# Index keys and query latents projected first, their norms and the gate chain run inside the in-projection

## The chip, the cores and the metric

The kernel runs on one core of one Trainium2 chip. Time is device microseconds (us) of one execution; the median of three runs is the metric. The engines are TensorE (PE; its weight loads are PEld), VectorE (DVE), ScalarE (ACT), GpSimd (POOL) and SyncE (SP, which issues the DMA transfers here).

## The reference, cut to what matters

One decoder layer over 512 tokens of width 1024. One input projection feeds two groups of heads:

```python
h = rms_norm(x, ln1_g[l])
proj = h @ w_in[l]
gq, gk, gv, gz, ga, gb, cq, ckv, kidx, widx = jnp.split(proj, offsets, axis=-1)
o_a = gdn_mixer(gq, gk, gv, gz, ga, gb, conv_w[l], a_log[l], dt_bias[l], gdn_norm_g[l])
o_b = dsa_mixer(cq, ckv, kidx, widx, q_norm_g[l], kv_norm_g[l], w_q_up[l], w_qidx_up[l],
                w_kv_up[l], idx_ln_g[l], idx_ln_b[l], rel_bias)
...
# gdn_mixer
qkv = jax.nn.silu(causal_depthwise_conv(jnp.concatenate([q, k, v], axis=-1), conv_w))
q = l2_normalize(q...); k = l2_normalize(k...)
g = -jnp.exp(a_log) * jax.nn.softplus(a + dt_bias)
beta = jax.nn.sigmoid(b)
o = gated_delta_rule(q, k, v, g, beta)
o = rms_norm(o, norm_g) * jax.nn.silu(z)
# dsa_mixer
cq = rms_norm(c_q, q_norm_g);  q_idx = (cq @ w_qidx_up);  ckv = rms_norm(c_kv, kv_norm_g)
k_idx = layer_norm(k_idx, idx_ln_g, idx_ln_b)
w_idx = w_idx * (IDX_HEADS ** -0.5 * IDX_DIM ** -0.5)
```

After these come the gated delta rule in chunks of 64, the index scores with a top-k choice, the attention, the output projection, and an expert network (PEER) that takes most of the time.

## The kernel before

The program is a row of blocks. All five engines enter a block together and leave it together; inside, each runs its own list in order, and semaphores join them. This case is about the first block (`in_stage`) and the start of the second (`mixer_stage`); everything behind is left alone.

`in_stage` computes 21 tiles of 128 output channels by 512 tokens. For tile `i` SP loads 512 KB of weights, ScalarE rounds them to a high part (`split(i)`, L212), VectorE makes the low part (`w_rest(i)`, L283), and TensorE runs three passes of 8 matmuls (L362, L374, L379). `split(i)` may start when tile `i-2` is done, since there are two weight buffers. Bank `i % 4` holds the result; ScalarE stores it (`store`, L216; the first four on VectorE, L287). The tile order is that of the rows of `proj`: tiles 0 to 11 are q, k, v of the delta rule, 12 to 15 its gate z, 16 to 19 the query and key/value latents (`CQ0`, `CKV0`), 20 the index keys together with the columns a, b and w_idx (`KI0`).

Between tiles the q, k, v rows are convolved on VectorE (`convolve`, L298 and L301), passed through Silu and squared on ScalarE (`convolved`), summed over partitions on TensorE (L386), given an inverse root by ScalarE's Ln and Exp (`roots`, L239 and L241) and scaled on VectorE (`normalise`, L305). Ln, Exp and Silu lie in three activation tables; a change between them is an ACT_TABLE_LOAD. Copy and Square need no load. Where a tile index matters: `roots(k)` waits for `normalise(2k-1)`, and TensorE waits for the Ln of `roots` before it reuses the banks of L386.

`mixer_stage` opens with a chain that needs tile 20 and the latents. TensorE transposes the index-key tile (L1147) and subtracts the mean (L1149); VectorE and ScalarE make from a and b the decay `g` and `beta` (L814 to L850); TensorE sums the squares of the four latents and of the centred keys (L1152 to L1155), multiplies the relative bias by the buckets (L1157, the `strip`), and sums `g` (L1159 to L1162, `cums`). Only then comes the loop over four heads: `row_sums(h)` (L1170 to L1173), `products(h)` (transposes L1181, then the 64-wide products L1189), the head's masks on VectorE (L886 to L892), the index projections `up_project` (L1227) and a transpose of the result (L1265). The norms of the latents and keys (L865 to L870) stand on VectorE inside the first head.

The head of TensorE's list in this block, in the code's own words:

```python
pe.wait_ge(s["rel"], 32)
mm(t.bank[0][0:H, :], rel[:], buckets[:, 0:T], start=True, stop=True).then_inc(s["strip"], 1)
...
pe.wait_ge(s["strip_s"], 2)
row_sums(0)
pe.wait_ge(s["llog"], 3)
products(0)
```

Of the kernel before, what the change touches and what calls it, by code (L numbers as in the profile page):

```python
# [27 lines left out]
P = 128  # L28
T = 512
# [24 lines left out]
NPROJ = 21  # L54
NEG = -1e30
# [107 lines left out]
def in_stage(t, a, x, proj, conv, hi, lo, x_hi, x_lo, sq, spare, parts):  # L163

    nc = t.nc
    LEAD = 4
    loaded = [t.sem(f"in_loaded{s}") for s in range(2)]
# [6 lines left out]
        t.sem("conv_" + k) for k in ("zeroed", "taps", "silu", "squared", "summed", "rooted", "inverted", "normed"))  # L176
    whi, wlo = (parts[:, k:k + 4, :].rearrange("p (s c) t -> p s (c t)", s=2) for k in (0, 4))
    raw = spare[:, 8:12, :].rearrange("p (s c) t -> p s (c t)", s=2)
    root, inv = spare[:, 12:14, :], spare[:, 14, :]
    slots = [proj[:, NPROJ - DC + c, PAD:PAD + T] for c in range(DC)]  # L180
# [4 lines left out]
    dest = lambda i: proj[:, i, PAD:PAD + T]  # L185
    bank = lambda i: t.bank[i % 4]
    with nc.Block() as block:

        @block.sync
        def _(sp):  # L190
# [10 lines left out]
            sp.dma_start(t.cst[:, rest], a["constants"][:, rest]).then_inc(rest_in, 16)  # L201
# [3 lines left out]
        def _(act):  # L205
# [24 lines left out]
            def gate(j):  # L230
                act.wait_ge(stored, j + 1)
                f(dest(j), dest(j), ACT.Silu).then_inc(silu, 1)

            def roots(k):
# [6 lines left out]
                f(both, both, ACT.Exp, scale=-0.5).then_inc(conv_inverted, 1)  # L241

# [21 lines left out]
            for i in range(6, NPROJ):  # L264
                u = i // 2
# [12 lines left out]
        def _(dve):  # L278
            tt, stt = nc.vector.tensor_tensor, nc.vector.scalar_tensor_tensor
# [13 lines left out]
            def convolve(j):  # L293
                dve.wait_ge(stored, j + 1)
                for tap in range(CONV):
                    w = v[:, V_CONV + j * CONV + tap:V_CONV + j * CONV + tap + 1]
                    if tap == 0:
                        nc.vector.tensor_scalar(conv[:, j, :], proj[:, j, 0:T], w, None, ALU.mult).then_inc(taps, 1)  # L298
                    else:
                        dve.wait_ge(taps, CONV * j + tap)  # L300
                        stt(conv[:, j, :], proj[:, j, tap:tap + T], w, conv[:, j, :], ALU.mult, ALU.add).then_inc(taps, 1)  # L301

            def normalise(j):
                dve.wait_ge(conv_inverted, j // 2 + 1)
                stt(conv[:, j, :], conv[:, j, :], v[:, V_QK + j:V_QK + j + 1], root[:, j % 2, :],  # L305
                    ALU.mult, ALU.mult).then_inc(conv_normed, 1)

# [22 lines left out]
            convolve(0)  # L330
            w_rest(5)
            store(3)
            convolve(1)
            for i in range(6, NPROJ):
# [5 lines left out]
            normalise(2 * H - 1)  # L340

# [7 lines left out]
        def _(pe):  # L349
            mm = nc.tensor.matmul  # L350
            for i in range(NPROJ):
                s = i % 2
                pe.wait_ge(w_high, i + 1)
# [5 lines left out]
                for c in range(DC):  # L359
                    if fresh:  # L360
                        pe.wait_ge(high_made, c + 1)
                    mm(bank(i)[:], whi[:, s, of_c[c]], highs[:, c, :], start=c == 0, stop=False)  # L362
                    if i == 0:
                        pe.wait_ge(low_made, c + 1)
                        mm(bank(i)[:], whi[:, s, of_c[c]], lows[:, c, :], start=False, stop=False)
                pe.wait_ge(w_low, i + 1)
                if i == 1:
                    pe.wait_ge(ones_in, 16)
                    for k in range(DC // 2):
                        pe.wait_ge(paired, k + 1)  # L370
                        last = mm(t.bank[4][:], t.c(C_ONES), sq[:, 2 * k + 1, :], start=k == 0, stop=k == DC // 2 - 1)
                    last.then_inc(added, 1)
                for c in range(DC):
                    last = mm(bank(i)[:], wlo[:, s, of_c[c]], highs[:, c, :], start=False, stop=i == 0 and c == DC - 1)  # L374
                if i:
                    for c in range(DC):
                        if fresh:
                            pe.wait_ge(low_made, c + 1)
                        last = mm(bank(i)[:], whi[:, s, of_c[c]], lows[:, c, :], start=False, stop=c == DC - 1)  # L379
                last.then_inc(summed, 1)  # L380
                j = i - 10
                if 0 <= j < 2 * H:
                    pe.wait_ge(conv_squared, j + 1)
                    if j >= 2:
                        pe.wait_ge(conv_rooted, j // 2)
                    mm(t.bank[6 + j % 2][:], t.c(C_ONES), sq[:, j, :], start=True, stop=True).then_inc(conv_summed, 1)  # L386
# [212 lines left out]
def mixer_stage(t, proj, conv, mix, hi, lo, qy, raw, front, tail, first_tiles, a_in):  # L599
# [11 lines left out]
        "chain", "ab_t", "ab", "exps", "u1", "log",  # L611
        "g", "beta", "below", "after", "cums", "g_col", "decays", "beg", "gl", "grow", "exp3", "tiles_t", "kk",
        "taken", "qk", "a", "a_t", "at", "prep", "mt", "x", "xs", "tx", "level", "u_t", "w_t", "u", "w", "zero",
        "ws", "vnew", "out", "o_copy", "ds", "state", "osq", "ossq", "olog", "oinv", "delta_mixed",
        "lsq", "mean", "centred", "csq", "lsum", "llog", "linv", "latents", "kin")}
    s.update({n: t.sem("dsa_" + n) for n in (
        "wqi", "wq", "wkv", "rel", "w_idx", "up", "up_out", "strip", "strip_s", "strip_out",
# [24 lines left out]
    with ExitStack() as ctx:  # L642
# [4 lines left out]
        ab = sb("ab", [P, NB, 8])  # L647
        small = sb("small", [P, 16, 16])
        ghalf = sb("ghalf", [P, 2, 16])
# [6 lines left out]
        w_idx = sb("w_idx", [P, NB, IH])  # L656
# [13 lines left out]
        gl, eg = tmp[:, 0, half0], up_q[:, 0, :]  # L670
# [4 lines left out]
        latent = [proj[:, CQ0 + i, PAD:PAD + T] for i in range(4)]  # L675
        keys_i = proj[:, KI0, PAD:PAD + T]
        sm = [small[:, i, :] for i in range(16)]
# [1665 lines left out]
```

## Time and profile before

| | before |
|---|---|
| median of 3 runs | 1635.97 us (1634.32 to 1637.51) |
| the profiled execution's own time | 1635.17 us |
| its span | 1633.4 us |
| mean granted TensorE clock | 0.990 |
| TensorE matmul busy | 1571.5 us (96%) |
| VectorE / ScalarE / GpSimd busy | 1301.6 / 701.4 / 604.4 us |

The span runs from the first instruction to the last; the 1.8 us beside it lie outside the trace. The in-projection fills the first 141 us, and the head loop of the mixer lies between 151 and 196 us. Rows of the timeline give the start, the duration of the merged piece, the engine, the line and the operation; in brackets stands how long the engine was idle before it and what ended that. Matmul durations overlap, so the distance between starts is the better price. A float32 matmul of the mixer appears as two records.

### The profile page before, as it was taken

How to read it: one execution, taken by the hardware profiler on the slowest of the kernel's cores; microseconds unless marked ns; L12 is line 12 of the kernel's file. 1: busy time of each engine (PE TensorE's matmuls, PEld its weight loads, DVE VectorE, ACT ScalarE, POOL GpSimd, SP SyncE). 2: the span in 40 equal slices, each digit the busy share in tenths (PEclk: the TensorE clock that was granted, in tenths of full speed). 3: DMA queues.
4: the chain of work that ended last, by engine and by line, in shares of the span. 5: the costliest groups of instructions: out<-in, count | busy, mean ns of one | idle time of the engine just before them, and what ended most of it. 6: DMA issues, size and time to landing. Idle time of an engine off the chain costs nothing.

```text
span 1633.4 us, 26769 instructions
## 1 busy us (share of the span) xinstructions
PE 1571.5 (96%) x9253; PEld 1362.2 (83%) x9253; DVE 1301.6 (80%) x2391; ACT 701.4 (43%) x1118; POOL 604.4 (37%) x447
## 2 busy tenths in 40 slices
PE   7998889879999999999999999999999999999997
PEld 5876576558789999999999999998888888888886
DVE  6844567876525989999999999758898989898887
ACT  6474357363433334343444444433333333333334
POOL 3000047155402678787533333223333333322220
PEclk9999999989999999999999999999999999999999
DMA  4321011002243588888899999999999999999995
GB/s 135 114 69 60 2 41 27 26 27 90 89 157 101 174 269 290 270 282 293 254 334 362 347 343 349 345 345 397 381 381 399 379 380 387 392 360 338 360 367 192
DMA packets 149112, 404.47 MB, mean 248 GB/s; under 512 B 14176, under 2 KB 71776, under 8 KB 145568
## 3 DMA queue, kind: packets, MB, share of 16 engines
q1 hardware_dynamic: 108704, 243.93, 43.7%
q0 software_dynamic: 36864, 134.23, 21.5%
q10 hardware_dynamic: 3456, 25.17, 3.7%
q8 instruction: 51, 0.84, 0.2%
q14 instruction: 37, 0.30, 0.0%
HBM read 350.77 MB, written 52.51 MB: 247 GB/s over the span
## 4 chain that ended last, share of the span: by engine, by line
PE 56%; DVE 11%; issue 1%; ACT 0%; DMA 0%; POOL 0%; DVEq 0%; ACTq 0%
PE bank L1614 32%; PE bank L2148 7%; PE bank L2152 7%; PE bank L2149 7%; DVE own_waste L1930 3%; PE bank L2170 3%; DVE back L1981 1%; DVE rt_num L1952 1%; DVE rt_num L1945 1%; DVE rt_work L1946 1%; DVE rt_pos L1974 0%; DVE rt_pos L1971 0%; DVE rt_cand L1964 0%; DVE back L2002 0%; DMA h<-u_rows_dram,own_experts 0%
## 5 line engine op out<-in xcount | busy, mean ns | idle before, releaser
L1614 PE MATMUL bank<-rt_u_parts,rt_w_hi 128*128 128x512 f32 x1536 | 369.1, 389 | 0.0
L2148 PE MATMUL bank<-hi_parts,rt_u_parts 128*128 128x384 f32 x1024 | 349.5, 341 | 0.0
L2149 PE MATMUL bank<-lo_parts,rt_u_parts 128*128 128x384 f32 x1024 | 342.4, 334 | 0.0
L1614 PEld LDWEIGHTS bank<-rt_u_parts,rt_w_hi 128*128 128x128 f32 x1536 | 288.1, 188 | 59.8
L1843 ACT ACTIVATE rt_u_parts<-raw 128x1024 fp32r<-128x1024 f32 x126 | 133.8, 1062 | 336.7 <-PE bank L2152 296.8
L1480 ACT ACTIVATE rt_u_parts<-raw 128x1024 fp32r<-128x1024 f32 x128 | 135.9, 1062 | 320.9 <-PE bank L1614 293.2
L2199 POOL DMA_INDIRECT h<-u_rows_dram,own_experts x128 | 177.3, 1385 | 224.2 <-DVE own_waste L1930 210.0
L2205 POOL DMA_INDIRECT qy<-v_dram,own_experts x128 | 130.9, 1023 | 347.3 <-DVE qy L1554 341.4
L1890 POOL TENSOR_TENSOR rt_u_parts<-raw,rt_u_parts 128x1024 fp32r<-128x1024 f32 x66 | 163.3, 2474 | 127.0 <-ACT rt_u_parts L1843 125.6
L1536 DVE TENSOR_TENSOR rt_u_parts<-raw,rt_u_parts 128x1024 fp32r<-128x1024 f32 x128 | 156.7, 1224 | 66.4 <-ACT rt_u_parts L1480 64.2
L2152 PE MATMUL bank<-hi_parts,rt_u_parts 128*128 128x384 f32 x1024 | 198.4, 334 | 1.2 <-DVE rt_u_parts L1923 1.2
L1614 PE MATMUL bank<-rt_u_parts,rt_w_lo 128*128 128x512 f32 x768 | 194.9, 389 | 0.0
L2149 PEld LDWEIGHTS bank<-lo_parts,rt_u_parts 128*128 128x128 f32 x1024 | 192.6, 188 | 0.0
L2148 PEld LDWEIGHTS bank<-hi_parts,rt_u_parts 128*128 128x128 f32 x1024 | 192.5, 188 | 0.0
L2152 PEld LDWEIGHTS bank<-hi_parts,rt_u_parts 128*128 128x128 f32 x1024 | 179.3, 188 | 1.5 <-DVE rt_u_parts L1923 1.5
L1614 PEld LDWEIGHTS bank<-rt_u_parts,rt_w_lo 128*128 128x128 f32 x768 | 144.1, 188 | 29.9
L1554 DVE SCALAR_TENSOR_TENSOR qy<-qy,own_weights 128x1024 f32<-128x1024 f32 x128 | 163.9, 1280 | 0.1
L1930 DVE SCALAR_TENSOR_TENSOR own_waste<-h,bank 128x1024 bf16<-128x1024 f32 x104 | 126.6, 1218 | 4.7 <-DMA h<-u_rows_dram,own_experts 2.0
L1923 DVE TENSOR_TENSOR rt_u_parts<-raw,rt_u_parts 128x1024 fp32r<-128x1024 f32 x60 | 73.5, 1226 | 31.4 <-ACT rt_u_parts L1843 31.4
L1536 DVE TENSOR_TENSOR rt_w_lo<-rt_w,rt_w_hi 128x384 fp32r<-128x384 f32 x128 | 70.6, 552 | 0.7 <-ACT rt_w_hi L1484 0.7
L480 DVE TENSOR_TENSOR conv_parts<-proj,conv_parts 128x1024 fp32r<-128x1024 f32 x22 | 32.7, 1485 | 48.0 <-ACT conv_parts L432 48.0
L1484 ACT ACTIVATE rt_w_hi<-rt_w 128x384 fp32r<-128x384 f32 x128 | 65.4, 511 | 11.5 <-DVE rt_w L1564 11.4
(361 smaller groups left out, 2340.7 us busy)
## 6 DMA issues: line engine op xcount, KB each, us to landing
raw<-u_dram SPq DMA_DIRECT2D x128, 512.0 KB
raw<-v_dram SPq DMA_DIRECT2D x128, 512.0 KB
active_scratch<-rt_act SPq DMA_DIRECT2D x128, 192.0 KB
gates_scratch<-front ACTq DMA_DIRECT2D x12, 1024.0 KB
gates_scratch<-back ACTq DMA_DIRECT2D x12, 1024.0 KB
front<-gates_scratch SPq DMA_DIRECT2D x8, 1536.0 KB
front<-active_scratch SPq DMA_DIRECT2D x64, 192.0 KB
back<-active_scratch SPq DMA_DIRECT2D x64, 192.0 KB
```

The source lines that it names most:

```text
L1480: nc.scalar.activation(v_hi[:, par, :], raw[:, j, :], ACT.Copy).then_inc(v_high, 1)
L1536: nc.vector.tensor_tensor(out, a, high.bitcast(F32), ALU.subtract).then_inc(done, 1)
L1554: nc.vector.scalar_tensor_tensor(own, ring[:, j, :], w_own[:, bass.ds(e, 1)], own, ALU.mult, ALU.add).then_inc(added, 1)
L1614: return mm(bank_of[b][z][:], left[:, b * P:(b + 1) * P], right[:, halves[z]], start=False, stop=stop)
L1843: a(u_hi[:, j % 2, :], raw[:, j % 4, :], ACT.Copy).then_inc(u_high, 1)
L1890: nc.gpsimd.tensor_tensor(u_lo[:, e % 2, :], raw[:, e % 4, :], u_hi[:, e % 2, :].bitcast(F32), ALU.subtract).then_inc(u_low, 1)
L1930: d.scalar_tensor_tensor(waste[:], ring[:, r, :], 1.0, h_tok[:], ALU.mult, ALU.mult, accum_out=dots[:, bass.ds(k, 1)]).then_inc(dot, 1)
L2148: mm(bank, u_hi[:, j % 2, chunk[c]], hi[:, c, 0:TD], start=c == 0, stop=False)
L2149: mm(bank, u_hi[:, j % 2, chunk[c]], lo[:, c, 0:TD], start=False, stop=False)
L2152: last = mm(bank, u_lo[:, j % 2, chunk[c]], hi[:, c, 0:TD], start=False, stop=c == DC - 1)
L2199: t.nc.gpsimd.indirect_dma_start(out=u_ring[:, k % RING, :], out_offset=None, in_=u_rows, in_offset=bass.IndirectOffsetOnAxis(ap=eidx[:, k ...
L2205: t.nc.gpsimd.indirect_dma_start(out=ring[:, k % RING, :], out_offset=None, in_=v_rows, in_offset=bass.IndirectOffsetOnAxis(ap=eidx[:, k:k ...
```

## The change

The weights of the in-projection are reordered on the host (`ROW_OF`): the index-key tile comes first, then the two query latents, the twelve q, k, v tiles, the two key/value latents, and the four z tiles last. In the same numbers as before, tile 0 is now the index keys, 1 and 2 the query latents, 3 to 14 q, k, v, 15 and 16 the key/value latents, 17 to 20 z. Everything of the mixer's opening chain except the strip moves into `in_stage`: the function `between` puts its matmuls into TensorE's list after a given number of products, and ScalarE and VectorE get the matching pieces between their tiles. The z tiles are stored through Silu directly. The rest of the constants is loaded after tile 3's weights, instead of after the last tile. In the mixer `products(0)` stands ahead of `row_sums(0)`, the strip matmul behind it, and `gl` has two buffers. The convolutions start three tiles later relative to the start, and `normalise` stands ahead of `convolve`.

```diff
+ROW_OF = (KI0, CQ0, CQ0 + 1) + tuple(range(QKV_T)) + (CKV0, CKV0 + 1) + tuple(range(Z0, Z0 + H))
...
+                if i == 3:
+                    sp.dma_start(t.cst[:, rest], a["constants"][:, rest]).then_inc(rest_in, 16)
...
-                f(dest(i), bank(i)[:], ACT.Copy).then_inc(stored, 1)
+                f(dest(i), bank(i)[:], ACT.Silu if i >= Z_AT else ACT.Copy).then_inc(stored, 1)
...
+            squares()
+            split(6)
+            store(4)
+            inverse_roots()
+            split(7)
+            store(5)
+            log_of_gate()
+            for i in range(8, NPROJ):
                 split(i)
                 store(i - 2)
-                if i - 6 < QKV_T:
-                    convolved(i - 6)
-                if Z0 <= i - 2 < Z0 + H:
-                    gate(i - 2)
-                if i % 2 and u < 6 + H:
-                    roots(u - 6) if u >= 6 else None
+                if 0 <= i - 9 < QKV_T:
+                    convolved(i - 9)
+                if i == 19:
+                    value_squares()
+                if i == 10:
+                    decay()
+                if i >= 14 and i % 2 == 0:
+                    roots((i - 14) // 2)
+                if i == 20:
+                    value_root()
...
+            take_gates()
+            w_rest(6)
+            first_gate_steps()
+            norm_latents()
+            for i in range(7, NPROJ):
                 w_rest(i)
-                if i - 4 < QKV_T:
-                    convolve(i - 4)
-                if 14 <= i:
-                    normalise(i - 14)
+                if i == 7:
+                    last_gate_steps()
+                if 0 <= i - 15 < 2 * H - 1:
+                    normalise(i - 15)
+                if 0 <= i - 7 < QKV_T:
+                    convolve(i - 7)
+                if i == 9:
+                    gate_columns()
...
+            def between(i, k):
+                if i == 4 and k == 0:
+                    pe.wait_ge(rest_in, 16)
...
+                elif i == 5 and k == 2:
+                    pe.wait_ge(csq_s, 1)
+                    mm(t.bank[4][:], t.c(C_SAME), csq, start=True, stop=True).then_inc(lsum, 1)
+                elif i == 8 and k == 3:
+                    pe.wait_ge(g_s, 1)
...
+                    if made[0] % 6 == 0 and i >= LEAD:
+                        between(i, made[0] // 6 - 1)
...
-                pe.wait_ge(s["strip_s"], 2)
+                products(0)
                 row_sums(0)
-                pe.wait_ge(s["llog"], 3)
-                products(0)
+                pe.wait_ge(s["rel"], 32)
+                mm(t.bank[7][0:H, :], rel[:], buckets[:, 0:T], start=True, stop=True).then_inc(s["strip"], 1)
```

TensorE, before: the opening of the mixer. `cst` are the constants, `gdn_small` the gate's small columns, `lo` holds `gl`, `raw` the buckets.

```order
L1147 MATMUL bank<-cst,proj 128x128 x4
L1149 MATMUL bank<-proj,cst 128x512
L1152 MATMUL bank<-proj,cst 128x512
L1153 MATMUL bank<-proj,cst 128x512
...
L1155 MATMUL bank<-proj,cst 128x512
L1157 MATMUL bank<-raw,gdn_rel 4x512
L1159 MATMUL bank<-gdn_small,cst 128x16
...
L1170 MATMUL bank<-lo,cst 128x4x64 x2
L1172 MATMUL bank<-lo,cst 128x256
L1173 MATMUL bank<-gdn_small,cst 128x256
L1181 MATMUL bank<-cst,conv 128x128 x8
L1189 MATMUL bank<-conv 64x2x64 x8
```

TensorE, after the change, at the same place:

```order
L1270 MATMUL bank<-cst,conv 128x128 x8
L1278 MATMUL bank<-conv 64x2x64 x8
L1259 MATMUL bank<-lo,cst 128x4x64 x2
L1261 MATMUL bank<-lo,cst 128x256
L1262 MATMUL bank<-gate_small,cst 128x256
L1338 MATMUL bank<-raw,gdn_rel 4x512
```

Ten matmuls and four transposes have left the place in front of the head loop; the strip matmul stands behind the first head's products and row sums.

TensorE, after the change, in tiles 4 and 5 of the in-projection (`hi_parts` and `lo_parts` are the two parts of the normalised input; L531 is the product, formerly L362, L374 and L379):

```order
L531 MATMUL bank<-hi_parts,qy_parts 128x512 x6
L500 MATMUL bank<-cst,proj 128x128 x4
L503 MATMUL bank<-proj,cst 128x512
L531 MATMUL bank<-hi_parts,qy_parts 128x512 x10
L531 MATMUL bank<-lo_parts,qy_parts 128x512 x8
...
L508 MATMUL bank<-proj,cst 128x512 x2
...
L531 MATMUL bank<-lo_parts,qy_parts 128x512 x2
L512 MATMUL bank<-proj,cst 128x512
L531 MATMUL bank<-lo_parts,qy_parts 128x512 x6
```

The transposes, the mean and the sums of squares now stand between products of these tiles. The four `cums` stand behind tile 8, two more sums of squares behind tile 19.

ScalarE, before, from `split(20)` to the end of the block (L212 is `split`, L216 `store`):

```order
L239 ACT_TABLE_LOAD
L239 ACTIVATE qy<-bank,vec 128x1024
L241 ACT_TABLE_LOAD
L241 ACTIVATE qy<-qy 128x1024
L212 ACTIVATE qy_parts<-qy 128x1024
L216 ACTIVATE proj<-bank 128x512 x3
```

ScalarE, after the change, from `split(20)` to the end (L238 is `split`, L242 `store`, L251 Silu, L261 and L263 `roots`, L302 and L304 the values' root):

```order
L238 ACTIVATE qy_parts<-qy 128x1024
L242 ACTIVATE proj<-bank 128x512
L251 ACTIVATE conv<-conv 128x512
L261 ACT_TABLE_LOAD
L261 ACTIVATE qy<-bank,vec 128x1024
L263 ACT_TABLE_LOAD
L263 ACTIVATE qy<-qy 128x1024
L302 ACT_TABLE_LOAD
L302 ACTIVATE proj<-bank,vec 128x512
L304 ACT_TABLE_LOAD
L304 ACTIVATE proj<-proj 128x512
L242 ACTIVATE proj<-bank 128x512 x2
```

The last pair of roots, the values' root and a table load for the Silu of the last two stores have moved behind the last split.

## Rows read from the trace of the kernel before

**Rows 1.** The page, the chain that ended last, by engine.

```profile
PE 56%; DVE 11%; issue 1%; ACT 0%; DMA 0%; POOL 0%; DVEq 0%; ACTq 0%
```

**Rows 2.** Timeline of TensorE in the in-projection: start, duration, engine, line.

```profile
71.09 1.98 PE L362 MATMUL bank<-hi_parts,qy_parts 128*128 128x512 f32 x8
...
76.53 1.02 PE L386 MATMUL bank<-h,cst 128*128 128x512 f32 x2
...
82.87 1.02 PE L386 MATMUL bank<-h,cst 128*128 128x512 f32 x2
...
104.18 1.10 PE L386 MATMUL bank<-h,cst 128*128 128x512 f32 x2 [2.13 <-ACT qy L239]
...
138.69 1.98 PE L379 MATMUL bank<-lo_parts,qy_parts 128*128 128x512 f32 x8
```

**Rows 3.** Timeline of ScalarE in the in-projection: a pair of roots, a store.

```profile
87.17 1.11 ACT L239 ACTIVATE qy<-bank,vec 128x1024 f32<-128x1024 f32 x1
88.31 1.28 ACT L241 ACT_TABLE_LOAD   x1
89.60 1.06 ACT L241 ACTIVATE qy<-qy 128x1024 f32<-128x1024 f32 x1
...
91.52 0.58 ACT L216 ACTIVATE proj<-bank 128x512 f32<-128x512 f32 x1
...
101.63 1.28 ACT L239 ACT_TABLE_LOAD   x1 [3.23 <-DVE conv L305]
```

**Rows 4.** Timeline of TensorE at the opening of the mixer.

```profile
141.60 0.63 PE L1147 MATMUL bank<-cst,proj 128*128 128x128 f32 x4 [0.94 <-PEq L187]
...
147.37 1.02 PE L1157 MATMUL bank<-raw,gdn_rel 32*4 32x512 f32 x2
148.32 0.40 PE L1159 MATMUL bank<-gdn_small,cst 128*128 128x16 f32 x2
...
149.01 0.37 PE L1162 MATMUL bank<-gdn_small,cst 128*128 128x16 f32 x2
151.32 2.04 PE L1170 MATMUL bank<-lo,cst 128*128 128x256 f32 x4 [1.94 <-DVE lo L853]
...
154.77 1.04 PE L1181 MATMUL bank<-cst,conv 128*128 128x128 f32 x8
155.74 1.09 PE L1189 MATMUL bank<-conv 128*64 128x128 f32 x16
158.12 1.13 PE L1170 MATMUL bank<-lo,cst 128*128 128x256 f32 x4 [1.29 <-DVE lo L853]
...
159.95 1.04 PE L1181 MATMUL bank<-cst,conv 128*128 128x128 f32 x8
...
164.70 5.40 PE L1227 MATMUL bank<-proj,hi 128*128 128x512 f32 x8
...
171.68 3.70 PE L1227 MATMUL bank<-proj,hi 128*128 128x512 f32 x8 [0.97 <-ACT proj L994]
```

**Rows 5.** Timeline of VectorE at the opening of the mixer.

```profile
149.08 0.17 DVE L843 MEMSET qy<- 4x128 f32 x1
...
161.81 0.69 DVE L886 TENSOR_TENSOR front<-conv,raw 128x512 f32<-128x512 f32 x1
...
163.21 0.41 DVE L892 TENSOR_TENSOR lo<-bank,raw 128x256 f32<-128x256 f32 x1
```

**Rows 6.** Windows: stretch, length, busy time of PE, PEld, DVE, ACT, POOL, PEclk, DMA, GB/s.

```profile
49.33:76.50 27.17, 27.17 (x121) 22.52 (x120) 21.58 (x29) 13.48 (x20) 0.00 (x0) 1.00 0.37 117
...
151.30:154.80 3.50, 3.48 (x9) 2.77 (x10) 0.00 (x0) 0.76 (x2) 0.00 (x0) 0.52 0.21 18
...
163.70:170.00 6.30, 6.30 (x24) 2.86 (x24) 3.18 (x6) 1.29 (x3) 0.73 (x1) 0.73 0.00 0
```

**Rows 7.** DMA issues up to 200 us: size, us from issue to landing.

```profile
cst<-constants_dram SPq DMA_DIRECT2D x1, 768.0 KB, 5.3
...
raw<-buckets_dram SPq DMA_DIRECT2D x1, 80.0 KB, 4.6
```

More of the change, by code:

```diff
@@ L176, in in_stage @@
         t.sem("conv_" + k) for k in ("zeroed", "taps", "silu", "squared", "summed", "rooted", "inverted", "normed"))
+    (chain_s, ab_t, ab_s, w_idx_s, mean, centred, lsq_s, csq_s, lsum, llog, linv, latents, kin) = (
+        t.sem("idx_" + k) for k in (
+            "chain", "ab_t", "ab", "w_idx", "mean", "centred", "lsq", "csq", "lsum", "llog", "linv", "latents", "kin"))
+    exps, u1_s, log, g_s, cums, g_col, decays = (t.sem("gate_" + k) for k in (
+        "exps", "u1", "log", "g", "cums", "g_col", "decays"))
     whi, wlo = (parts[:, k:k + 4, :].rearrange("p (s c) t -> p s (c t)", s=2) for k in (0, 4))
@@ L179, in in_stage @@
     root, inv = spare[:, 12:14, :], spare[:, 14, :]
-    slots = [proj[:, NPROJ - DC + c, PAD:PAD + T] for c in range(DC)]
+    slots = [proj[:, H + c, PAD:PAD + T] for c in range(DC)]
     v = t.vec
@@ new lines, in first_gate_steps, with norm_values @@
+            def first_gate_steps():
+                dve.wait_ge(exps, 3)
+                ts(early.u1, early.z, 1.0, None, ALU.add).then_inc(u1_s, 1)
+                dve.wait_ge(u1_s, 1)
+                link(ts(early.eq, early.u1, 1.0, None, ALU.is_equal))
+                link(stt(early.rat, early.u1, -1.0, early.eq, ALU.add, ALU.add))
+                link(nc.vector.reciprocal(early.rat, early.rat))
+                link(tt(early.rat, early.rat, early.z, ALU.mult))
+            def norm_values():
+                dve.wait_ge(linv, 3)
+                for c in range(2, 4):
+                    stt(latent[c], latent[c], v[:, V_QN + c:V_QN + c + 1], log_inv[2], ALU.mult, ALU.mult).then_inc(latents, 1)
@@ new lines, in norm_latents @@
+            def norm_latents():
+                dve.wait_ge(linv, 1)
+                for c in range(2):
+                    stt(latent[c], latent[c], v[:, V_QN + c:V_QN + c + 1], log_inv[0], ALU.mult, ALU.mult).then_inc(latents, 1)
+                dve.wait_ge(linv, 2)
+                stt(keys_i, keys_i, v[:, V_IG:V_IG + 1], log_inv[1], ALU.mult, ALU.mult).then_inc(kin, 1)
+                dve.wait_ge(kin, 1)
+                ts(keys_i, keys_i, v[:, V_IB:V_IB + 1], None, ALU.add).then_inc(kin, 1)
@@ L674, in mixer_stage @@
         am = (up_q[:, 3, half0], up_q[:, 3, half1])
-        latent = [proj[:, CQ0 + i, PAD:PAD + T] for i in range(4)]
         keys_i = proj[:, KI0, PAD:PAD + T]
-        sm = [small[:, i, :] for i in range(16)]
-        xa, nx, z, u1, lnu, eq, rat, sp_, g, ebb, beta, gcol, eg_col, egam, beg, ea = sm
-        g_neg = nx
         row = lambda r: proj[:, r, 0:T]
@@ L683, in mixer_stage @@
         lat = proj[:, CQ0:CQ0 + 4, PAD:PAD + T]
-        lsq, csq, log_inv = [row(i) for i in range(4)], row(4), [row(i) for i in (8, 9, 10)]
         up_idx = [row(j) for j in range(NIDX)]
@@ L882, in _ @@
                     else:
-                        norm_latents()
+                        take_strip()
                     dve.wait_ge(s["exp3"], 3 * (h + 1))
```

278 lines of the change are left out of this document (146 added, 132 removed).

## The prediction

> **What bounds the kernel now.** I read the chain that ended last first. It lies on TensorE for 56% of the span and on VectorE for 11% [rows 1], and its lines belong to the expert stages, which the change leaves alone. So the change can only shift everything behind it, and the question is how early the mixer's head loop gets going. I therefore went through the timelines of TensorE, ScalarE and VectorE up to 200 us, looking for what TensorE waits for.
>
> In the in-projection TensorE is the limit. A tile takes 5.44 us (71.09 to 76.53), a tile with one float32 sum behind it 6.34 us (76.53 to 82.87), so such a sum costs 0.90 us [rows 2]. There is one wait worth the name, 2.13 us at 104.18, for the Ln of `roots(1)`. Its cause is on ScalarE: that pair of roots started only at 101.63, after 3.23 us of waiting for a `normalise` [rows 3] which VectorE has behind a convolution. In five ordinary tiles VectorE is busy 21.58 us and ScalarE 13.48 us of 27.17 [rows 6]; both have room, TensorE has none. The last product starts at 138.69 and takes 1.98 [rows 2].
>
> The opening of the mixer is different. TensorE's first instruction there is at 141.60, and the first index projection `up_project(0)` starts at 164.70, 23.1 us later [rows 4]. What TensorE does between them is small: it follows a chain that goes back and forth with VectorE and ScalarE, and ends in row sums that wait 1.94 us for `gl` and run 3.45 us instead of the second head's 1.83 us (151.32 to 154.77, against 158.12 to 159.95) [rows 4], at a granted clock of 0.52 in that stretch, mostly the 1.2 GHz level [rows 6]. After `up_project(0)` the engine is nearly always busy until 196 us, so I take that instruction as the mark: what it gains, the end gains.
>
> **Part 1, the in-projection gets longer.** Moved into it are four transposes, bounded by the merged row of 0.63 us, four `cums`, 1.06 us from the first start to the last end (148.32 to 149.01 plus 0.37) [rows 4], and six float32 matmuls of 512 columns (mean, two query sums, the keys' sum, two value sums) at the 0.90 us found above [rows 2], 5.4 us. The sum is 7.1 us if each pays for its own start; back to back they overlap a little, and I take 6.9 us. It is real cost, because TensorE was the limit there. Before, the same matmuls cost about the same but lay in the opening; they come off in part 3.
>
> **Part 2, the wait at 104.18 goes.** `roots(k)` now stands at even tiles from 14, and `normalise` stands ahead of the convolution. From the end of tile 14: ScalarE needs a split of about 1 us and a store of 0.58 us [rows 3], then Silu and square, and meets a `normalise` that VectorE finishes after `w_rest`, about 3 us in. Load and Ln of 1.28 + 1.11 us [rows 3] put the Ln's end near 5.4 us, and TensorE asks for it 6.34 us in. Nothing waits: minus 2.1 us. The margin is near 0.9 us, so this is a term that could come back in part.
>
> Of the new waits in this block the closest are these. The transposes wait for the constants, now issued behind tile 3's weights at about 16 us; the same transfer took 5.3 us [rows 7], and with 512 KB ahead of it I expect it some 10 us before it is asked for. `split(7)` stands behind the two inverse roots, and the second waits for the keys' sum three quarters through tile 5. From that sum ScalarE needs an Ln, a table load and two Exps, near 3.2 us; it is asked for about 7 us after the sum (a quarter of tile 5 and all of tile 6). Behind it on VectorE stands `w_rest(7)`, behind the norms of the latents (about 2.6 us), asked for 1.8 us later still, with 2 us to spare. At the end, `split(20)` on ScalarE is followed by store, Silu, the last roots, the value root and a table load for the z stores. From the end of tile 18 I count 3.0 us until `normalise(5)`, 4.7 for the roots, 1.3 for a load and 0.6 for the Ln (the value sums are there at 8.1 us), 1.9 for load and Exp, 1.9 for load and store: 13.4 us. TensorE ends tile 20 at 0.9 + 5.44 + 1.8 + 5.44 = 13.6 us. So the block still ends with one store of 0.58 us behind TensorE [rows 3], as before. That is free by 0.2 us only; if ScalarE is later, each us counts.
>
> Here the rule of the Trainium skill bears, page ScalarE: Activation LUTs, section What ACT_TABLE_LOAD costs: a switch is a load of about 1283 ns and a drain of about 1380 ns. The load in this trace takes 1.28 us; the drain is not there: Ln ends at 88.28, the load starts at 88.31, the Exp at 89.60 [rows 3]. The five loads behind `split(20)` would cost 6.9 us more by the page, and nothing by the rows.
>
> **Part 3, the opening.** Let M be TensorE's first instruction in the mixer. Products of the first head take 0.97 + 1.09 us (154.77, 155.74), row sums 1.83 us at full clock [rows 4], so TensorE is through at M + 3.9. What is late next is the strip. Its buckets are issued only when the block opens and land 4.6 us after their issue [rows 7]; before, the strip matmul started at 147.37, M + 5.77, right behind that landing [rows 4]. I keep that. The strip's copy and memset end at 149.25, 1.88 us behind its matmul [rows 5]. VectorE has nothing else open then: row sums were done at M + 4, the exponentials follow within 1.5 us, and the head's three tile products on VectorE ended near M + 3. So at M + 7.65 it starts L886 to L892, 1.81 us (161.81 to 163.62) [rows 5], which gives M + 9.5. TensorE meanwhile does the strip (0.95), row sums(1) (1.83) and the transposes (0.97) [rows 4] and is through at M + 9.5 as well. The 64-wide products and `up_project(0)` then follow as before, 1.08 us later (163.62 to 164.70): M + 10.6, against M + 23.1. Minus 12.5 us. VectorE's 3.8 us of latent norms between 157.98 and 161.81 are in that; they are now in the projection, under its slack.
>
> **Part 4, the clock.** Before, the first pair of index projections took 5.40 us, the next 3.70 us [rows 4]; the granted clock from 163.7 to 170 was 0.73 on average [rows 6], behind idle stretches. If TensorE's only idle time after M is the 1.9 us before the strip, the first pair should take 3.7 us: minus 1.7 us.
>
> **The sum.** 6.9 - 2.1 - 12.5 - 1.7 = -9.4 us. The profiled execution's own time is 1635.17 us, giving 1625.8; the median of the runs is 0.8 us above it, giving 1626.6. I say 1626.5. A change of 0.2% (3.3 us) is about what a measurement of this kernel can tell from none.
>
> **The rivals.**
> (a) The clock falls again. TensorE idles some 1.8 us before the strip; before, 1.94 us of idleness preceded the half-speed row sums, while 2.13 us at 104.18 and 1.29 us at 158.12 preceded no slower piece [rows 2, 4]. If it falls, row sums(1) take 1.6 us more, strip and transposes 0.7: the sum is -7.1, 1628.8 us. I give 0.25.
> (b) The projection stalls at one of the narrow places: the wait of 2.1 us returns, or ScalarE ends late by 1 to 3 us. The gain is 5 to 8 us, 1628 to 1631 us. 0.12.
> (c) Table switches cost more than their 1.28 us where they come densely: the queue behind `split(20)` has 0.2 us to spare and five loads, so every further us per load is five at the block's end; at 1.4 us more each the gain is 2.7 us, 1633.3 us. It is what the page's drain would give. The rows speak against it. 0.02.
> (d) The gain is lost further back, because the head loop's later heads or the state loop wait for something that did not move: the time stays at 1634 to 1637. For it: the strip's transfers and the weights that SP issues in the mixer are on their own clock. Against: all are issued from this block's events and move with it. 0.04.
> (e) Slower. VectorE's `w_rest(7)` stands behind `norm_latents`, which waits for ScalarE, which waits for a matmul in the middle of tile 5. With about 2 us to spare, whatever it is late beyond that stops TensorE in tile 7 and shifts all behind. It decides for slower only when the chain is late by 2 + 9.4 + 3.3 = 15 us; at 17 us late the time would be 1641. Nothing in the rows is of that size. 0.03.
>
> **The numbers.** The forecast itself has 0.54, with 1624.5 to 1628 as its own range (part 1 between 6.5 and 7.1, the spread of medians about 1.5). Below it some room is left if insertions overlap more or the strip lands sooner. The range goes from 1623.5 to 1630.5 and takes in (a) and most of (b). Faster by over 0.2%: 0.54 + 0.25 + 0.12 less its tail, 0.89; within 0.2%: (c), (d) and that tail of 0.02, 0.08; slower: (e), 0.03.
>
> **What would show it.** After: no idle of TensorE over 0.5 us in the projection after tile 4; its end near 145.5; the first instruction of the mixer near 146.4; the strip matmul 5.8 us behind it; `up_project(0)` near M + 10.6 and a first pair of 3.7 us. The prediction fails if the block's end is set by ScalarE's stores, if the strip's landing is later than before, or if the row sums of head 1 run at half clock.

## The result and the profile after

| | before | after |
|---|---|---|
| median | 1636.31 us (1633.88 to 1640.24, 8 runs) | 1626.35 us (1623.86 to 1632.13, 8 runs) |
| profiled execution, own time / span | 1635.17 / 1633.4 us | 1628.61 / 1626.8 us |

The ratio is 0.9942, with a 95% interval from 0.9925 to 0.9960: 10.0 us less by the medians, 6.5 to 12.3 by the interval. The prediction was 1626.5 us.

The timeline of TensorE after the change, tiles 4 and 5 of the projection, one later tile pair, and the projection's end; it answers to [rows 2]:

```profile
37.79 1.69 PE L531 MATMUL bank<-hi_parts,qy_parts 128*128 128x512 f32 x6 [0.81 <-ACT qy_parts L238]
39.31 0.60 PE L500 MATMUL bank<-cst,proj 128*128 128x128 f32 x4
...
46.08 1.88 PE L508 MATMUL bank<-proj,cst 128*128 128x512 f32 x4
...
105.39 1.02 PE L571 MATMUL bank<-h,cst 128*128 128x512 f32 x2
...
111.73 1.02 PE L571 MATMUL bank<-h,cst 128*128 128x512 f32 x2
...
137.09 1.88 PE L522 MATMUL bank<-proj,cst 128*128 128x512 f32 x4
...
142.48 1.98 PE L531 MATMUL bank<-lo_parts,qy_parts 128*128 128x512 f32 x8
```

The bracket of 2.13 us that stood at 104.18 in [rows 2] is gone; the tiles with one sum between them are 6.34 us apart (105.39 to 111.73), and there is no bracket between tile 4 and the end at 144.46. The opening of the mixer on TensorE, which answers to [rows 4]:

```profile
145.50 1.07 PE L1270 MATMUL bank<-cst,conv 128*128 128x128 f32 x8 [1.05 <-PEq L212]
146.50 1.09 PE L1278 MATMUL bank<-conv 128*64 128x128 f32 x16
147.52 1.13 PE L1259 MATMUL bank<-lo,cst 128*128 128x256 f32 x4
...
150.72 1.01 PE L1338 MATMUL bank<-raw,gdn_rel 32*4 32x512 f32 x2 [1.21 <-DMA raw<-buckets_dram]
151.67 1.13 PE L1259 MATMUL bank<-lo,cst 128*128 128x256 f32 x4
...
154.47 1.09 PE L1278 MATMUL bank<-conv 128*64 128x128 f32 x16
155.49 3.70 PE L1314 MATMUL bank<-proj,hi 128*128 128x512 f32 x8
159.12 0.68 PE L1351 MATMUL bank<-cst,raw 64*64 64x64 f32 x16
160.78 3.70 PE L1314 MATMUL bank<-proj,hi 128*128 128x512 f32 x8 [0.97 <-ACT proj L1124]
```

The first index projection (L1314, formerly L1227) starts 9.99 us after the block's first instruction, against 23.10, and its pair takes 3.70 us, against 5.40. What TensorE waits for is named in the row of 150.72: the buckets.

The end of the projection on ScalarE, whose room the prediction put at 0.2 us:

```profile
138.87 1.28 ACT L302 ACT_TABLE_LOAD   x1
140.16 0.69 ACT L302 ACTIVATE proj<-bank,vec 128x512 f32<-128x512 f32 x1
140.87 1.28 ACT L304 ACT_TABLE_LOAD   x1
142.16 0.63 ACT L304 ACTIVATE proj<-proj 128x512 f32<-128x512 f32 x1
142.81 1.28 ACT L242 ACT_TABLE_LOAD   x1
144.11 1.08 ACT L242 ACTIVATE proj<-bank 128x512 f32<-128x512 f32 x2
145.46 1.28 ACT L1157 ACT_TABLE_LOAD   x1 [0.27 <-PEq L212]
```

ScalarE has no gap from 138.87 on; the block ends with its second store at 145.19, 0.7 us behind TensorE.

**What the profiled pair doesn't show of the gain.** The two spans differ by 6.6 us, the medians by 10.0. The windows between four marks (first product of the level loop, first sum of squares of the delta output, first product of the output projection, first low product of the expert stage) say where. Columns as in [rows 6]. Before:

```profile
195.80:315.30 119.50, 112.10 (x1420) 80.79 (x1421) 92.86 (x200) 65.41 (x153) 50.38 (x53) 1.00 0.09 24
315.30:348.80 33.50, 19.81 (x69) 12.37 (x69) 27.02 (x64) 21.28 (x62) 17.25 (x19) 0.69 0.13 46
348.80:504.10 155.30, 149.29 (x689) 121.80 (x688) 76.97 (x92) 57.32 (x91) 47.60 (x35) 1.00 0.29 97
```

After:

```profile
184.90:305.60 120.70, 113.40 (x1420) 82.24 (x1421) 93.04 (x200) 65.43 (x153) 50.40 (x53) 0.99 0.08 23
305.60:338.90 33.30, 19.33 (x69) 11.93 (x68) 26.79 (x64) 21.61 (x62) 17.90 (x19) 0.74 0.13 46
338.90:497.00 158.10, 152.10 (x688) 124.21 (x687) 77.16 (x93) 57.10 (x91) 47.35 (x35) 0.98 0.29 97
```

At the level loop the changed kernel is 10.9 us ahead (195.8 to 184.9). The first stretch then takes 1.2 us longer and the third 2.8, with the same instructions and a lower clock (0.99 and 0.98 against 1.00 on average). Behind 504.1 and 497.0 the two are alike to 0.5 us (1129.3 and 1129.8 us). Nothing in the change forces this: experiments 7 and 8, which keep it, have 155.3 us again in the third stretch, and 8 has 119.5 in the first. Both traces of the changed kernel itself have the longer values, though, and why is left open.

### The profile page after: what moved, and what is told of

It reads as the page before. It is cut to its first block, busy times and chain, and to the rows that moved or that the text cites. A ratio compares the mean times of both kernels' runs of the same rounds, so it can differ in the third digit from the quotient of the medians.

```text
span 1626.8 us, 26773 instructions
## 1 busy us (share of the span) xinstructions
PE 1571.8 (97%) x9253; PEld 1364.1 (84%) x9253; DVE 1300.7 (80%) x2391; ACT 710.5 (44%) x1122; POOL 604.6 (37%) x447
## 3 DMA queue, kind: packets, MB, share of 16 engines
q0 software_dynamic: 36864, 134.23, 21.5%
## 4 chain that ended last, share of the span: by engine, by line
PE 56%; DVE 11%; issue 1%; ACT 0%; DMA 0%; POOL 0%; DVEq 0%; ACTq 0%
PE bank L1700 32%; PE bank L2234 7%; PE bank L2235 7%; PE bank L2238 7%; DVE own_waste L2016 3%; PE bank L2256 3%; DVE back L2067 1%; DVE rt_num L2038 1%; DVE rt_num L2031 1%; DVE rt_work L2032 1%; DVE rt_pos L2060 0%; PE bank L2216 0%; DVE rt_pos L2057 0%; DVE back L2088 0%; DMA h<-u_rows_dram,own_experts 0%
```

## The experiments

Distances read from TensorE's timeline in each profiled execution: the mixer's first instruction M, the way from M to the first index projection, and the duration of that pair, in us. The ratio is to the kernel before, run beside it. Tile 4 of the projection starts at 37.2 to 38.6 us in these traces, and M moves with it. "By marks" below means by such starts in the timelines, and not by the runs' times.

| kernel | M | M to projection | pair | ratio (95%) |
|---|---|---|---|---|
| before | 141.60 | 23.10 | 5.40 | |
| before, second trace | 142.36 | 23.14 | 5.40 | |
| after | 145.50 | 9.99 | 3.70 | 0.9942 (0.9925 to 0.9960) |
| after, second trace | 145.53 | 9.94 | 3.70 | |
| before, products first | 140.82 | 18.80 | 3.70 | 0.9965 (0.9954 to 0.9976) |
| before, normalise first | 138.68 | 21.44 | 5.40 | 0.9982 (0.9971 to 0.9994) |
| before, filler | 141.94 | 22.32 | 4.39 | 0.9975 (0.9962 to 0.9988) |
| before, three small edits | 138.67 | 18.81 | 3.70 | 0.9949 (0.9935 to 0.9964) |
| after, two more loads | 148.52 | 11.85 | 3.70 | 0.9965 (0.9953 to 0.9976) |
| after, keys' sum late | 151.87 | 10.15 | 3.70 | 0.9975 (0.9959 to 0.9991) |
| after, buckets first | 145.53 | 9.30 | 3.70 | 0.9924 (0.9903 to 0.9945) |
| after, transposes first | 144.88 | 8.81 | 3.70 | 0.9918 (0.9903 to 0.9932) |

**1. One part alone: the products ahead of the row sums.**

```diff
-                row_sums(0)
                 pe.wait_ge(s["llog"], 3)
                 products(0)
+                row_sums(0)
...
-        gl, eg = tmp[:, 0, half0], up_q[:, 0, :]
+        gl, eg = (tmp[:, 0, half0], tmp[:, 0, half1]), up_q[:, 0, :]
```

> The kernel before, with one part of the change alone: the first head's products stand ahead of its row sums, and gl has two buffers; the chain stays in the opening of the mixer. My theory: the opening was long because each step waited for the one before, and the products filled none of the gaps. TensorE's 1.94 us of idleness at 149.4 is filled by 2 us of products, the row sums run at full clock, VectorE does the head's tile products before the latent norms. VectorE then sets the pace (tile products to 153.1, norms to 157.3, masks to 159.1), so the first index projection starts 18.6 us after the block opens instead of 23.1, and its pair takes 3.7 instead of 5.4 us: 5 to 6 us less in all, 1630 us. Rival (the whole chain has to leave the opening before anything is gained): only TensorE's own 2 us come off, 1634 us.

Measured: 18.80 us and 3.70, ratio 0.9965, 5.7 us less by the ratio. TensorE's timeline:

```profile
148.52 1.09 PE L1181 MATMUL bank<-cst,conv 128*128 128x128 f32 x8
...
150.56 1.13 PE L1170 MATMUL bank<-lo,cst 128*128 128x256 f32 x4
...
154.06 1.10 PE L1170 MATMUL bank<-lo,cst 128*128 128x256 f32 x4 [1.50 <-ACT raw L1054]
...
158.60 1.09 PE L1189 MATMUL bank<-conv 128*64 128x128 f32 x16 [1.70 <-DVE lo L892]
159.62 3.70 PE L1227 MATMUL bank<-proj,hi 128*128 128x512 f32 x8
```

The gap of 1.94 us is filled, the row sums run at full clock, and what is late next are VectorE's masks of head 0. The rival falls: with the whole chain still in place more than half of the gain is there.

**2. One part alone: the order of `normalise` and `convolve`.**

```diff
-                if i - 4 < QKV_T:
-                    convolve(i - 4)
                 if 14 <= i:
                     normalise(i - 14)
+                if i - 4 < QKV_T:
+                    convolve(i - 4)
```

> The kernel before, with normalise(i - 14) ahead of convolve(i - 4) on VectorE, nothing else. My theory: the one wait of 2.1 us of TensorE in the projection (before the sum behind tile 14) goes, the last product of the projection starts at 136.6 instead of 138.7 and the time falls by about 2 us (1634 us, near the limit of what can be told). Rival (the wait comes from the table loads of the roots, not from the order on VectorE): the wait stays at about 2 us.

The wait is gone: the sum behind tile 14 stands without a bracket.

```profile
37.74 2.12 PE L362 MATMUL bank<-hi_parts,qy_parts 128*128 128x512 f32 x8 [0.84 <-ACT qy_parts L212]
...
101.34 1.02 PE L386 MATMUL bank<-h,cst 128*128 128x512 f32 x2
...
135.76 1.98 PE L379 MATMUL bank<-lo_parts,qy_parts 128*128 128x512 f32 x8
...
148.39 1.10 PE L1170 MATMUL bank<-lo,cst 128*128 128x256 f32 x4 [1.94 <-DVE lo L853]
...
160.12 5.40 PE L1227 MATMUL bank<-proj,hi 128*128 128x512 f32 x8
```

The median fell by 3.5 us, the ratio says 1.0 to 4.7. The row at 148.39 is of interest for the clock: the same 1.94 us of idleness, and here the first four row-sum records take 1.10 us, not 2.04 as in [rows 4]; that alone shortens the opening by 1.7 us.

**3. Two matmuls in the gap.**

```diff
+                for _ in range(2):
+                    mm(t.bank[7][:], ones, lsq[0], start=True, stop=True)
                 pe.wait_ge(s["strip_s"], 2)
                 row_sums(0)
```

> The kernel before, with two float32 matmuls of 512 columns into an unused bank in TensorE's list just ahead of the first row sums, where it was idle for 1.94 us; their result is not used. My theory: the idle stretch is what lets the clock fall, so the row sums take 1.8 us instead of 3.45 and the exponentials of head 0 come 1.6 us earlier. But VectorE is busy with tile products and norms until 161.8 us in any case after the transposes, and these come 1.6 us earlier too: the first index projection starts 1.6 us earlier, 21.5 us after the block opens. Total about 1.5 us less if nothing else falls. Rival (the clock falls for what TensorE did before the idle stretch, or at random): row sums stay near 3.4 us and the fillers only lengthen the list.

The row sums run at full clock (151.64 to 153.44, 1.8 us). The opening took 22.3 us, not 21.5: the second fall of the clock, which before came during the index projections, now came one instruction earlier, in the 64-wide products of head 1, which took 1.98 us instead of 1.09. By marks the gain to the end of the first pair is 1.8 us (with 0.3 us of a later start); the ratio says 2 to 6 us. The experiment alone doesn't tell the theory from the rival, since number 2 shows full-speed row sums with the gap open.

**4. Three small edits, the chain left in place.** The edits of 1 and 2, and the order of the transfers as in 7.

> The kernel before with three small edits and the chain left in the mixer: normalise ahead of convolve, the first head's products ahead of its row sums with two gl buffers, bias and buckets issued ahead of the index weights. My theory: most of the change's gain comes from filling gaps, not from moving the chain. The wait of 2.1 us in the projection goes, the opening shrinks from 23.1 to about 18 us (18.8 with the products alone, and the sums of g no longer stand behind a late strip), the first pair of index projections takes 3.7 instead of 5.4 us: 8.5 to 9 us less, 1629 us, against 9.9 for the change. Rival (the gains overlap, since the gap that one fills is the gap that the other shortens): 6 us less, 1632 us.

Measured: 1629.15 us, 8.8 us under the runs of before beside it (1637.94), ratio 0.9949. The two parts add up: M is at 138.67 and the projection 18.81 us behind it. The interval overlaps that of the whole change, and by marks (the end of the first pair, 161.1 against 159.1) the change is 2 us ahead. The third edit gained nothing here (18.81 against 18.80 with the products alone), where I had expected 0.8 us: TensorE was busy with the sums until it reached the strip matmul at 144.44, and the chain through `g` was no faster.

```profile
143.49 1.02 PE L1155 MATMUL bank<-proj,cst 128*128 128x512 f32 x2
144.44 1.02 PE L1157 MATMUL bank<-raw,gdn_rel 32*4 32x512 f32 x2
```

That is M + 5.77, and in all six traces with the chain in place the strip matmul stands at M + 5.76 or 5.77. Here the buckets had landed at M + 2.6 already (issued at M + 0.35, 2.2 us on the way). So before the change the landing did not set this place.

**5. Two more table loads behind the last roots.**

```diff
                 if i == 20:
+                    f(early.lnu[:, 0:1], v[:, V_EPS:V_EPS + 1], ACT.Silu)
+                    f(early.lnu[:, 1:2], v[:, V_EPS:V_EPS + 1], ACT.Exp)
                     value_root()
```

> The changed kernel with two more table switches on ScalarE between the last roots and the values' root (a one-column Silu and a one-column Exp, results unused). My theory: ScalarE's queue behind split(20) has no room left, so the block ends later by what the two loads and the two small activations take, 2 x 1.28 + about 0.3 = 2.9 us, and the mixer opens that much later behind the last product (3.9 us instead of 1.0). Rival (a switch also costs a drain of 1.38 us, the rule of the Trainium skill, page ScalarE: Activation LUTs, section What ACT_TABLE_LOAD costs): 5.6 us later. Second rival (the queue has room): nothing.

TensorE's timeline, with 4.05 us between the blocks instead of 1.05:

```profile
142.50 1.98 PE L533 MATMUL bank<-lo_parts,qy_parts 128*128 128x512 f32 x8
148.52 1.94 PE L1272 MATMUL bank<-cst,conv 128*128 128x128 f32 x8 [4.05 <-PEq L212]
150.39 1.97 PE L1280 MATMUL bank<-conv 128*64 128x128 f32 x16
152.29 1.92 PE L1261 MATMUL bank<-lo,cst 128*128 128x256 f32 x4
```

3.0 us, as two loads of 1.28 and two small activations cost; there is no drain, and the rival's 5.6 us are off. ScalarE has no room left there. A second cost came with it, unforeseen: behind 4.05 us of idleness the products and row sums ran at the 1.2 GHz level (1.94 against 1.07 us for L1270's work), the opening took 1.9 us more, and the first index projection started 4.9 us later than in the changed kernel (160.37 against 155.49), not 2.9. The medians differ by 5.0 us, the ratios by 3.8.

**6. The keys' sum behind tile 6.**

```diff
-                elif i == 5 and k == 2:
+                elif i == 6 and k == 3:
```

> The changed kernel with the keys' sum of squares behind tile 6 instead of three quarters through tile 5. ScalarE's second Ln then waits for it, and split(7) and w_rest(7) stand behind that. My theory (in the projection TensorE pays for every us by which the queue behind the chain exceeds its margin): the sum comes at 58.2 to 59.1 us, Ln, load and two Exps take 3.1 us, split(7) 1 us, so TensorE waits about 3.9 us before tile 7, and about 1 us more in it for w_rest(7) behind the latent norms: 4 to 5 us slower than the change, 1631 us. Rival (later tiles absorb it, since all engines but TensorE have room): the wait shows in tile 7 but the end of the projection stays within 1 us of 144.5.

```profile
56.71 1.02 PE L512 MATMUL bank<-proj,cst 128*128 128x512 f32 x2
61.92 6.43 PE L531 MATMUL bank<-hi_parts,qy_parts 128*128 128x512 f32 x16 [4.19 <-ACT qy_parts L238]
68.19 2.00 PE L531 MATMUL bank<-lo_parts,qy_parts 128*128 128x512 f32 x8
...
148.85 1.98 PE L531 MATMUL bank<-lo_parts,qy_parts 128*128 128x512 f32 x8
```

TensorE waited 4.19 us (3.9 expected), and nothing of it was absorbed: the last pass starts at 148.85, 6.4 us later than in the changed kernel, and 7.0 us later if counted from the start of tile 4, which came 0.6 us earlier here (37.20 against 37.79). The edit itself moved the keys' sum by 6.8 us (counted the same way, 19.5 against 12.7), so about 2.5 us of room were used up before TensorE waited; the median is 6.1 us above that of the change, the ratios differ by 5.4 us. The missing part is again the clock. Sixteen products took 6.43 us, where the changed kernel needs 3.79 for them. The windows of this run:

```profile
60.00:61.90 1.90, 0.00 (x0) 0.00 (x0) 1.38 (x3) 1.90 (x4) 0.00 (x0) 0.63 0.00 0
61.90:64.00 2.10, 2.08 (x5) 1.70 (x6) 2.06 (x4) 2.07 (x4) 0.00 (x0) 0.50 0.00 0
64.00:66.00 2.00, 2.00 (x6) 1.51 (x6) 1.79 (x9) 1.31 (x2) 0.00 (x0) 0.50 0.30 61
```

The extra microsecond for `w_rest(7)` that I expected did not show; it ended at 64.25, and the first eight products at half clock took longer than that.

**7. The buckets ahead of the index weights.**

```diff
-                sp.dma_start(wqi, a_in["w_qidx_up"]).then_inc(s["wqi"], 16)
                 sp.dma_start(rel[:], a_in["rel_bias"]).then_inc(s["rel"], 16)
                 sp.dma_start(buckets, a_in["buckets"]).then_inc(s["rel"], 16)
+                sp.dma_start(wqi, a_in["w_qidx_up"]).then_inc(s["wqi"], 16)
```

> The changed kernel with the bias and bucket transfers issued ahead of the 1 MB of index weights. My theory: what is late in the opening now is the strip, which waits for the buckets behind those weights. They land about 2.5 us after the block opens, TensorE's 1.2 us of idleness goes, the strip matmul starts 4.0 us after the opening instead of 5.2, and the first index projection starts 9.0 instead of 10.0 us after it, limited then by the masks behind the exponentials of head 0. Total 1 us less, not to be told apart by the time alone. Rival (the opening is bounded by the exponentials and masks, not by the strip): the projection still starts 10.0 us after.

The buckets land 2.1 us after their issue instead of 4.4, the strip matmul starts at M + 3.94, the projection at M + 9.30. The next limit is the one named in the row:

```profile
149.47 1.02 PE L1338 MATMUL bank<-raw,gdn_rel 32*4 32x512 f32 x2
151.04 1.10 PE L1259 MATMUL bank<-lo,cst 128*128 128x256 f32 x4 [0.56 <-ACT raw L1160]
```

So the strip was what was late, but by 0.7 us and not 1.0; behind it stand the exponentials, which free the row sums' banks.

**8. Transposes ahead of the row sums, buckets first.** `products` is cut in two, `turned(h)` (the transposes) and the rest, and each later head runs `turned`, `row_sums`, `products`; the first keeps its products ahead of its row sums.

```diff
+                turned(0)
                 products(0)
                 row_sums(0)
...
+                        turned(h + 1)
                         row_sums(h + 1)
                         products(h + 1)
```

> The changed kernel with the buckets first and, in each head, the transposes ahead of the row sums. My theory: TensorE has then work while the exponentials of head 0 run; order products, row sums, strip, transposes of head 1, row sums of head 1; the first index projection starts 8.6 to 9.0 us after the opening (10.0 in the changed kernel, 9.0 with the buckets first alone), the later heads are bounded by TensorE and gain nothing. Total 1 to 1.5 us less than the change, near 1625. Rival (the transposes ahead delay the row sums of the later heads and with them the exponentials): the second pair of index projections starts later than 5.3 us after the first.

M + 8.81, as expected, and the pairs stand 5.29 us apart as in the change. 1623.97 us, ratio 0.9918: the fastest kernel of the study, though its interval overlaps that of the change. Of its 2.4 us over the change some 1.2 are in these rows, the rest is not separated from what the clock does.

**9. The two kernels once more.**

> The changed kernel once more, a second trace. My theory: up to the first index projection it repeats within 0.3 us (opening 10.0 us, strip matmul 5.2 us after the block opens), and what differs between the two traces is where the granted clock lies at the 1.2 GHz level in the stages from 183 to 500 us, so the span differs by 1 to 5 us. Rival (the changed kernel's runs spread because the opening depends on when the buckets land): the opening differs by more than 1 us.

> The kernel before once more, a second trace. My theory: the opening repeats (23.1 us, the first pair of index projections 5.4 us) and the stages from 183 to 500 us differ from the first trace by where the granted clock lies at the 1.2 GHz level, so that the distance from the first index projection to the first product of the expert stage (336.5 us in the first trace) moves by 1 us or more. Rival (the clock follows the program alone): the falls come at the same instructions and that distance repeats within 0.3 us; then the 3 us by which the changed kernel's profiled execution fell short of the medians' difference need another cause.

The openings repeat to 0.05 us. The changed kernel's second trace repeats also the later stretches (120.70, 33.30 and 158.10 us again), so for it the theory that the clock's falls vary from trace to trace is not borne out. The kernel before does not repeat: the same three stretches took 120.8, 33.9 and 156.4 us where the first trace had 119.5, 33.5 and 155.3, and from the first index projection to the expert stage's mark it is 342.2 us against 339.4 (the 336.5 in the expectation is a slip). Its second trace has this window in the level loop, and the first trace at the same place the one below it:

```profile
196.00:199.00 3.00, 2.41 (x46) 2.44 (x48) 2.31 (x7) 0.79 (x3) 0.00 (x0) 0.61 0.00 0
```

```profile
196.00:199.00 3.00, 2.90 (x99) 2.79 (x97) 2.26 (x7) 1.53 (x4) 0.00 (x0) 1.00 0.02 5
```

The same program, the same wait in front (1.98 us for VectorE's mask), and once the level products run at half speed, once not. That wait of 1.98 us stands ahead of the level loop in all twelve traces of the study: the first 64 products behind it took 2.4 us in five of them and 2.8 to 3.6 us in seven.

The projection of the kernel before does not repeat either. Behind the wait of 2.13 us that part 2 of the prediction is about, the second trace has

```profile
103.33 1.10 PE L386 MATMUL bank<-h,cst 128*128 128x512 f32 x2 [2.13 <-ACT qy L239]
103.87 3.79 PE L362 MATMUL bank<-hi_parts,qy_parts 128*128 128x512 f32 x8
```

and the first

```profile
104.71 2.41 PE L362 MATMUL bank<-hi_parts,qy_parts 128*128 128x512 f32 x8
```

From 105.5 to 107.5 us the granted clock of the second trace was 0.50, the 1.2 GHz level, and from the first product of tile 4 to M it took 104.93 us, against 103.31: 1.6 us for the same instructions and the same wait.

## Why the prediction was right

**Part 1, the longer projection (6.9 us).** From the first product of tile 4 to the last product's end the projection took 106.67 us (37.79 to 144.46), before 102.38 (38.29 to 140.67). Experiment 2, which takes away the wait alone, has 100.00 (37.74 to 137.74). So the moved matmuls cost 6.7 us. Two float32 sums back to back cost hardly less than two single ones: the last pass of tile 20 starts 5.39 us behind the start of the two (137.09 to 142.48), against 4.52 us behind one (105.39 to 109.91), so the second cost 0.87 us. The block change took 0.1 us more (1.05 against 0.94).

**Part 2, the wait of 2.1 us.** Gone in the change and, by the same edit alone, in experiment 2. The cause was the order on VectorE, as said, not the table loads, which experiment 2 leaves as they were. It was worth 2.4 us (102.38 against 100.00): the bracket of 2.13 us is less than the delay, since the sum came at 104.18, 2.3 us behind its place in the row of 6.34 us steps (101.89). And experiment 9 shows that it could cost 1.6 us more by the clock.

**Part 3, the opening (12.5 us).** Measured 13.1. The strip was what was late next (experiment 7), but came at M + 5.22 instead of 5.77: the buckets landed 4.4 us after an issue at M + 0.81. The prediction had read 5.77 as "right behind that landing" and kept it. That reading was wrong: before, the landing was at M + 5.4 (0.81 + 4.6), and experiment 4 shows the same M + 5.77 with the buckets there 3 us earlier. TensorE reached the strip through its own sums. The term was off by only 0.55 us because the two places lie so close, which is luck. From the strip matmul to the first index projection TensorE has no gap, as forecast, and needs 4.77 us, against the 4.8 reckoned.

My working gave no share to the two causes. Experiments 1 and 4 do: 4.3 us of the 13.1 come from putting the products into a gap, and that edit also brings the 1.7 us of part 4. The move of the chain itself, with the strip matmul put behind the row sums, shortens the opening by another 8.8 us (18.80 to 9.99) and pays 6.7 us in the projection; the 2 us left are what the change is ahead of experiment 4. No run moves the chain and leaves the row sums first, so the shares hold for this order of the edits.

**Part 4, the clock (1.7 us).** Exact as a size, 5.40 to 3.70. As a reason it was half right. The pair ran slowly in the four traces (both of before, experiments 2 and 3) where TensorE had waited 2.69 us for VectorE shortly before, and at full speed in all others, where the wait there was 1.70 us or less; gaps of 4.05 and 4.19 us brought the 1.2 GHz level too (experiments 5 and 6). But the same gap did not always do the same: 1.94 us did so in two traces of before and not in experiment 2, 2.13 us in one trace of the four that have this wait, 1.98 us in seven traces of twelve. The length of the gap alone does not decide it, and what does is left open. The rival (a) therefore was a fair one, and its argument that 2.13 us at 104.18 preceded no slower piece held for that trace and not for the second one. It did not come at the strip, whose wait was 1.2 us; it came instead at 185 us, in the level loop, where the profiled change lost 1.2 us again.

**The sum.** At the end of the first pair (L1265, now L1351) the change is ahead by 170.03 - 159.12 = 10.9 us, 0.5 of them from an earlier start of tile 4, so 10.4 are the change's; forecast were 9.4. By the terms: 6.7 + 0.1 - 2.4 - 13.1 - 1.7 = -10.4. The medians say 10.0. That the forecast time was within 0.2 us of the median is partly luck: part 1 cost 0.2 us less than forecast, parts 2 and 3 gained 0.3 and 0.6 more, the block change took 0.1 back, and the later stages give and take up to 4 us by the clock. In the twelve profiled executions of the study the way from the level loop to the expert stage's mark lies between 307.9 and 312.1 us.

**The rivals.** (b) did not come, though ScalarE's end is as narrow as said: experiment 5 closes it, and all of the 3.0 us past it are paid, plus the clock; its other place, the wait of part 2, no experiment closed. Experiment 6 closes the place that (e) names, the queue behind the keys' sum, which had about 2.5 us of room. (c), the drain, is excluded by experiment 5. (d) did not show as a wait for something left behind: what the profiled pair lost further back, 3.8 us, were the same instructions at a lower clock. (e) did not show. That a long idle stretch costs more than itself was missing from (b) and (e): 3 us late at the block's end cost 4.9.

## What to carry to other kernels

Before a chain is moved under a busy engine, look whether the waiting engine has work of its own that stands behind the wait. Here an exchange of two calls and a second buffer, together with one exchange on VectorE, gave 8.8 us where the whole change gave 10.0 (the two intervals overlap), since the move pays in full (6.7 us) for the matmuls that it puts into a stage bound by TensorE. Small transfers that a chain waits for belong ahead of the large one in the same queue: this gave 0.7 us in the changed kernel, and nothing in experiment 4, where TensorE was not waiting for them.

A wait of TensorE of about 4 us is to be priced with the slower products behind it: 3.0 us more became 4.9, and 4.2 became 7.0 here, read from the timelines.

## What was unexpected of the hardware

The granted clock did not follow the program alone. 1.94 us of idleness ahead of the same row sums was followed by records of 2.04 and 1.84 us in two traces and of 1.10 us in a third. 2.13 us of idleness in the midst of a fully busy projection was followed by the 1.2 GHz level in one trace and by full clock in three others that run the same work up to there (3.79 against 2.40 to 2.42 us for the eight products behind the sum). Two traces of one kernel differed by 2.8 us over 340 us for it, and by 1.6 us in the projection. A difference of 1 to 3 us between two profiles therefore needs the clock's windows beside it before it is put down to an edit.

80 KB landed 2.1 us after their issue when they stood ahead of a transfer of 1 MB from the same engine, and 4.4 us when they stood behind it.
